# Two more passages between layers: the first half's squares of h added in pairs on GpSimd, the pairs summed on TensorE

## What is computed

```python
h = h + rmsnorm(y, g_post)        # y: output of the block
u = rmsnorm(h, g_pre)             # input of the next block
# rmsnorm(x, g) = x * rsqrt(mean(x * x, axis=-1) + EPS) * g
```

## Time and profile before

| | |
|---|---|
| median of 3 runs | 1691.23 us (1691.15 to 1692.78) |
| span of the profiled execution | 1689.5 us |
| TensorE busy | 1673.6 us, 99% of the span |
| VectorE busy | 1047.3 us, 62% |
| ScalarE busy | 739.1 us, 44% |
| GpSimd busy | 187.3 us, 11% |

### The profile page before, as it was taken

The page is one execution under the profiler, slowest core; times in us unless marked ns, Lnnn a source line. Parts: engine busy times, 40 slices in busy tenths (PEclk is TensorE's granted clock), DMA queues, the critical chain, the costliest instruction groups (busy, mean ns, idle before and its releaser), DMA issues.

```text
span 1689.5 us, 23254 instructions
## 1 busy us (share of the span) xinstructions
PE 1673.6 (99%) x9421; PEld 1404.4 (83%) x9421; DVE 1047.3 (62%) x1565; ACT 739.1 (44%) x1137; POOL 187.3 (11%) x163
## 2 busy tenths in 40 slices
PE   9999999999999999999999999999999999999998
PEld 7787887987898888888888888888898888888887
DVE  7889787474389449549675642655574545454445
ACT  6654467653553323213543323323364645253463
POOL 0455461200200000000100000000100000000001
PEclk9999999999999999999999999999999999999999
DMA  6111134421223223322322313313222222222221
GB/s 216 62 43 63 51 101 135 137 78 50 75 67 121 100 75 113 101 86 100 119 88 80 96 56 106 100 57 112 69 72 76 75 76 87 75 87 76 85 77 50
DMA packets 45576, 147.67 MB, mean 87 GB/s; under 512 B 5024, under 2 KB 8992, under 8 KB 45472
## 3 DMA queue, kind: packets, MB, share of 16 engines
q1 hardware_dynamic: 45472, 146.21, 26.5%
HBM read 144.09 MB, written 2.10 MB: 87 GB/s over the span
## 4 chain that ended last, share of the span: by engine, by line
PE 88%; DVE 8%; ACT 2%; issue 1%; DMA 0%; POOL 0%; SPq 0%; DVEq 0%; ACTq 0%
PE ps L502 22%; PE ps L504 22%; PE ps L503 22%; PE ps L507 21%; DVE sl L2052 1%; DVE ps L2112 1%; DVE y L2467 1%; DVE xl L2484 1%; DVE h L2477 0%; PE ps L1128 0%; ACT sh L1307 0%; DVE ps L2262 0%; DVE ps L2106 0%; DVE pad L2104 0%; DMA raw<-in_wqkv 0%
## 5 line engine op out<-in xcount | busy, mean ns | idle before, releaser
L1307 ACT ACTIVATE sh<-raw 128x1024 fp32r<-128x1024 f32 x257 | 268.3, 1053 | 373.1 <-PE ps L504 254.4
L2052 DVE TENSOR_TENSOR sl<-raw,sh 128x1024 fp32r<-128x1024 f32 x257 | 321.6, 1258 | 131.5 <-ACT sh L1307 131.4
L502 PE MATMUL ps<-xh,sh 128*128 128x512 f32 (+1 forms) x664 | 263.1, 396 | 0.0
L504 PE MATMUL ps<-xl,sh 128*128 128x512 f32 (+1 forms) x664 | 254.0, 382 | 0.0
L503 PE MATMUL ps<-xh,sl 128*128 128x512 f32 (+1 forms) x664 | 253.7, 382 | 0.0
L502 PE MATMUL ps<-sh,xh 128*128 128x512 f32 x384 | 151.8, 395 | 0.0
L503 PE MATMUL ps<-sh,xl 128*128 128x512 f32 x384 | 149.6, 390 | 0.0
L504 PE MATMUL ps<-sl,xh 128*128 128x512 f32 x384 | 149.6, 390 | 0.0
L502 PEld LDWEIGHTS ps<-xh,sh 128*128 128x128 f32 x664 | 124.9, 188 | 26.2 <-issue 2.4
L504 PEld LDWEIGHTS ps<-xl,sh 128*128 128x128 f32 x664 | 124.8, 188 | 24.9
L503 PEld LDWEIGHTS ps<-xh,sl 128*128 128x128 f32 x664 | 125.0, 188 | 22.7 <-issue 0.7
(11 more groups left out here) (429 smaller groups left out, 3317.5 us busy)
## 6 DMA issues: line engine op xcount, KB each, us to landing
raw<-in_wup SPq DMA_DIRECT2D x44, 512.0 KB, 3.5
raw<-in_wdn SPq DMA_DIRECT2D x24, 512.0 KB, 3.5
raw<-in_rqk SPq DMA_DIRECT2D x16, 512.0 KB, 3.9
raw<-in_rv SPq DMA_DIRECT2D x16, 512.0 KB, 3.4
raw<-in_rg SPq DMA_DIRECT2D x16, 512.0 KB, 4.4
raw<-in_rout SPq DMA_DIRECT2D x16, 512.0 KB, 3.5
raw<-in_sv SPq DMA_DIRECT2D x16, 512.0 KB, 3.4
raw<-in_sg SPq DMA_DIRECT2D x16, 512.0 KB, 3.5
```

Of the source, the lines that this page charges most:

```text
L502: e.matmul(dst, wh, ah, start=start, stop=False, skip_group_check=True)
L504: return e.matmul(dst, wh, al, start=False, stop=stop, skip_group_check=True)
L1307: e.activation(SH[j % NSPL][:], RAW[j % NRAW][:], ACT.Copy).then_inc(*hi(j))
L2052: e.tensor_tensor(SL[j % NSPL][:], RAW[j % NRAW][:], SH[j % NSPL][:].bitcast(F32), ALU.subtract).then_inc(*lo(j))
```

## The change

One table line is changed, and the code around it is as it was:

```diff
-        H_PAIR = {1: (1, 3, 5, 7), 2: (1, 3, 5, 7), 3: (), 4: ()}
+        H_PAIR = {b: (1, 3, 5, 7) for b in range(1, 5)}
         H_ADD = {1: (1, 2, 3, 4, 5, 6, 7), 2: (1, 2, 3, 4, 5, 6, 7), 3: (1, 3, 5, 7), 4: ()}
```

## The result

The changed kernel took 1695.74 us in the median (1693.96 to 1700.57, 16 runs), the kernel before 1691.76 us beside it (1691.13 to 1696.87, 16 runs). The ratio is 1.0021 with a 95% interval of 1.0014 to 1.0028: slower by 0.2%, 2.4 to 4.7 us. Set on the 1691.23 of the first table the ratio gives 1694.8. The profiled execution has a span of 1692.9 against 1689.5 us, +3.4. The lowest times are 2.8 us apart, the medians 4.0.

A forecast was written before the change was run, and what follows sets the result against it. VectorE was taken to pace TensorE early in passages 3 and 4, TensorE being late elsewhere; +1.53 and +1.45 us made +2.98, so 1694.2 us from 1691.2, range 1690.9 to 1695.5.

The forecast's parts named there:

- rival (a): GpSimd holds VectorE for the whole add, 0.67 at each of seven visible stretches: +4.5, 1695.7 us; over +3.4: chance 0.24.
- What bounds the passages: Passages 3 and 4: VectorE paces TensorE up to the second half's step 1; behind it TensorE is late.
- What is removed, 3.5 us: Eight first-half sums of 0.44 us go from TensorE in passages 3 and 4, a gain only where TensorE is late.
- What is added, 0.48 to 0.54 an add: Four GpSimd adds a passage, each stretching the VectorE instruction beside it by 0.48, or 0.54 on a weight split.
- The first add of passage 4, 0.15: Only the end of this add reaches VectorE's weight split, costing 0.15 us, an estimate between 0 and 0.54.
- Passage 3, +1.53: 0.55 us late at `y_sums`, 0.54 from the add on the weight split, 0.44 from the moved sum.
- Passage 4, +1.45: VectorE 1.65 us late, less 0.56 of slack at the second half's step 1, plus 0.36 for the moved sum.
- The sum, +2.98: Passages 3 and 4 together, +1.53 and +1.45 us, taking 1691.2 to 1694.2 us, 0.18% longer.
- Rival (b): In passages 3 and 4 the adds do not hit VectorE: 0 and -0.2, 1691.0 us; with partial hits, chance 0.14.
- (c): TensorE is the bound all through and the removed 3.5 us come in full: 1687.7 us, chance 0.03.
- (d): The change doesn't do what it says, pairs are not formed, nothing moves: 1691.2 us, chance 0.02.

The follow-up runs named there:

- e4: Changed kernel without GpSimd's adds in passages 3 and 4, TensorE summing only the even first-half blocks: median 1692.95 us, ratio 1.0006 to the kernel before.
- e6: Changed kernel with the same pair additions made by VectorE instead of GpSimd in passages 3 and 4: median 1694.68 us, ratio 1.0016 to the kernel before.
- e7: Kernel before with second-half additions on VectorE, seven in passage 3 (before four) and four in passage 4 (before none): median 1689.84 us, ratio 0.9986.
- e1: Kernel before with the change's pairs in passage 3 alone, passage 4 as before: lowest 1692.61 us, median 1694.23, ratio 1.0012.
- e10: Kernel before with the change's pairs in passage 4 alone, asked again in eleven runs: lowest 1692.66 us, median 1696.12, ratio 1.0018.
- e3: Kernel before plus GpSimd's eight adds into an unread tile, ScalarE's second-half squares waiting for them, all sums at old places: median 1695.38 us, ratio 1.0020.
- e2: Kernel before with the change's pairs in passage 4 alone, six runs: lowest 1693.52 us, median 1696.01, ratio 1.0024.
- e5: Kernel before plus GpSimd's eight adds each made twice into unread tiles, five runs: lowest 1696.99 us, median 1697.94, ratio 1.0042.

## Why the prediction was right, point by point

The ratio gives 1694.8 us for the 1694.2 forecast. That is +3.5 us, just past the +2.0 to +3.4 that had the largest chance; the range held because it takes in most of rival (a), and the bare median of 1695.74 is 0.2 above its end. The mechanism is right, as follows, and one term is missing, the clock.

- **What bounds the passages.** Right. VectorE paces TensorE up to the second half's step 1: e4 removes TensorE's work there and gains nothing, e6 gives VectorE 0.34 us more work an add and loses 2.2 us. Behind that step TensorE is late: e7 removes seven sums there and gains 2.9.
- **What is removed, 3.5 us.** The size was right (e7: 2.9 for seven, 0.42 each), and the place was where it counts for nothing.
- **What is added, 0.48 to 0.54 an add.** Right, by its rows: 0.94 to 0.96 against 0.47, 1.75 against 1.22. The Trainium skill's rule (SBUF — State Buffer, "Who interferes with whom"), read as a hold for the whole of the add, would have made it 0.67, and no row of the passages shows that. Wrong was which instruction pays. The prediction named as a sign of being wrong that the additions of h are not held, and they are not, in any row: the add for block 3 did not fall on the addition of h (834.68, 0.41) but on the `xl` behind it (835.02, 0.95; in passage 4 at 1250.85): GpSimd's row is 1.13 long instead of 0.80, it waited instead. And in passage 4 the last add fell on `x2lu` (1258.30), not on the weight split. None of that moved the sum, since the next instruction of VectorE, in strict order, lost the same time; the argument of rival (a) that two-input tensor_tensor steps besides the split are hit harder has no row in these passages either.
- **The first add of passage 4, 0.15.** It was 0.21 (1.43 against 1.22).
- **Passage 3, +1.53.** With the clock up, right: e1's lowest is +1.5. In the profiled execution the passage cost 2.21 (851.50 against 849.58, and the 0.29), by rows: at `y_sums` +1.33 for +0.55 (839.56 against 838.52), of which the slow step 3 is 0.78; at the restart +1.25 for +0.55; at step 1 +1.78 for +1.09. So 0.78 is the dip, less 0.08 that the walk overlooked: `y_sums` no longer stands behind a sum, and its first row is shorter (0.60 against 0.68). No other term is off.
- **Passage 4, +1.45.** Measured 1.47 (1265.57 against 1262.18, less 1.92), and e10's lowest is +1.6. The terms inside: the second half's step 1 is 0.96 late for 1.09, for VectorE made up 0.13 of its own idle time at an `xh`, and the moved sum costs 0.51 for 0.36. Two sums in a row take 0.80 (1264.32 to 1265.12) where one took 0.36 (1261.38 to 1261.74), so nothing is shared, 0.44; and the step now starts behind a wait, its first matmul taking 0.19 instead of 0.12.
- **The sum, +2.98.** The shortest four runs of the changed kernel are 1693.96 to 1694.43, 2.9 to 3.4 us over 1691.07. The median lies 1.3 to 1.8 higher than these: that is the clock, which the prediction had not as a term. It is a term of size: the mechanism forecast is 3.0 of the 3.4 in the spans, the dip is 0.7 of it less the 0.29 at the start. It carried the ratio just past the 0.2% that was forecast as the less likely side. That the point came so near, 0.6 us off, owes something to the ratio: the medians are 4.0 apart.
- **Rival (a), the whole add.** The time came out in its direction but not by its mechanism: no stretch of 0.67 is in the rows. By the prediction's own terms it passes 3.4 us from 0.51 a stretch (7 x 0.51 - 0.17), not from 0.54. **Rival (b)** is excluded by the stretched rows of both passages and by e3, **(c)** by e4, **(d)** by the 80 records.

**What stays open** is the dips. They stand behind waits of TensorE in passage 3 (the changed kernel, e1, e3) and in passage 4 (e2), and with TensorE fully busy at 116 to 124 us (e3, e4, e7, e10) and 212 to 220 us (e10). A wait is not enough for one: e5 and e6 wait for VectorE in passage 3 too, e6 up to 1.29 us, and have none. By medians the two passages do not add up: passage 4 alone lies 4.3 us (e2) and 4.5 us (e10) above the kernel before, more than the 4.0 of both passages together, so the +1.45 holds for executions with the clock up only. Whether the change makes them more frequent isn't settled: within 1 us of its own lowest lie 5 of 16 runs of the changed kernel and 41 of 75 of the kernel before, but e7, which adds no wait, has only 3 of 11, and e4, without adds, 2 of 11.

## What to carry to other kernels

Ask in which stretch the engine that gets relief is the late one; the same edit saves 0.9 us in a passage where TensorE is late and costs 1.5 where VectorE is, within one loop and in one kernel. Work handed to GpSimd beside a VectorE without idle time wasn't parallel here: count each such instruction as time of VectorE, from stretched rows of the same loop. Work removed from the wrong stretch (e4) is worth nothing, removed a few steps later (e7) it is worth all of its time.

## What the runs showed of the hardware

- GpSimd's add of 128x256 takes 0.8 us of its own and 0.48 to 0.54 of VectorE's where an instruction with both tensors in SBUF is beside it for long enough (0.21 at 1246.91, where it is only the add's end; none in VectorE's idle time, and `y<-y,ps` is not held). Two adds in a row take that twice (e5: 0.96 and 0.95 for 0.47). VectorE does such an add in 0.34.
- Who waits depends on who is under way: with VectorE's addition of h next in line, GpSimd's add took 1.13 us (834.56) and the addition its usual 0.41.
- TensorE's clock stood at 1.2 GHz for some 3 to 7 us in single places of single executions. With two dips where TensorE was busy throughout, e10 was 3.3 us late at passage 3, with one e3, e4 and e7 were 1.4 to 1.5, and those without between 0.3 early and 0.8 late; in passage 3 a dip of 3.4 us cost only 0.7, since the waits for VectorE took up the rest. The kernel before has runs near 1691.3 and then near 1692.8 to 1693.1, some 1.6 us apart; that this step is one such dip is likely but not shown, as no profile of one of the slower was taken.
